# The last two channels of the last down projection in two parts, prompt tokens first

## The chip, the core and the metric

The kernel runs on one NeuronCore of one Trainium2 chip. The metric is the device time of one execution in microseconds (us), first to last instruction and what lies around them. The time before is 2729.76 us, the median of three runs (2729.69 to 2732.67). Lower is better.

## The reference, cut to what matters

One step of a two-layer recurrent decoder with model width 2048. The kernel handles 336 tokens at once: 16 learned meta tokens and 256 prompt tokens (one sequence), and 64 sample tokens (8 sequences of 8). Each layer ends with a gated convolutional feed-forward, and the whole with an RMSNorm over the 2048 channels of a token. The change touches only these last lines:

```python
def conv_ffn(x, buf, g, w_up, w_gate, cw, cb, w_down):
    h = rmsnorm(x, g)
    up = h @ w_up
    upc, new_buf = causal_dwconv(up, buf, cw, cb)
    act = jax.nn.gelu(upc) * (h @ w_gate)
    return x + act @ w_down, new_buf
...
    y = rmsnorm(x, g_final)        # y = x * g / sqrt(mean(x*x) + eps), per token
```

The outputs of concern are `y_prompt` (256 x 2048; meta tokens have no output) and `y_sample` (64 x 2048), float32, 2.1 MB and 0.5 MB.

## The kernel before, in words

Activations lie transposed: `X` has 128 partitions x 16 channel groups ("channels" 0 to 15, each 128 model channels) x 336 tokens. In the token axis columns 0 to 15 are meta (`META` = 16), 16 to 271 prompt (`TP` = 272) and 272 to 335 samples (`T` = 336).

**Matmuls.** Each weight tile is loaded, rounded by ScalarE into `wh` (the high part, fp32r), and VectorE makes the low part `wl`. A product is then three matmuls per 128x128 block: `wh` by high activations, `wh` by low ones, `wl` by high ones (`tile`, L1654 to L1656), each with its own weight load. `RING` = 4 tiles are held at once.

**The last down projection** (`down12`) takes the last 14 blocks of the hidden width, in eight bodies of four tiles; body i makes channels 2i and 2i+1. Tiles j = 0 and 1 are the first seven blocks for the even and the odd channel, j = 2 and 3 the last seven. So a tile has 21 matmuls, and the matmuls of this layer run over columns 16 to 335 (320 tokens). The order on each engine is the order in which the code issues it: no planner, only semaphores between engines.

**Beside it, the output.** When channel c is complete VectorE adds it to `X` (`add_to_x`, L1332). GpSimd squares it and adds the squares to `ssq` (L913, L914; channel 15's squares are made by VectorE in `sql`, L1630). ScalarE multiplies it by the final gain into `yg` (L707), TensorE transposes `yg` in three windows of 128 tokens (`to_tokens`, L1943; windows start at tokens 16, 144 and 208, the last holding the samples in its upper 64 rows), and ScalarE copies the result to `yo` (tokens in partitions, L710).

**The end, in order.** After the last tile TensorE transposes channel 14, sums `ssq` and then `sql` over partitions by matmuls with `ones` (L2101, L2104: per window one column), and transposes channel 15. VectorE makes 1/(mean + eps) (L1632, L1633), ScalarE the root (L896). Then the rows of `yo` are scaled in six pieces, `PIECES` 0 to 5: (window 0, first half of the columns), (0, second half), (1, first), (1, second), (samples, first), (samples, second). VectorE scales pieces 0, 1, 4 (L1638), ScalarE 2, 3, 5 (L901). SyncE issues one store per piece, in the order 0, 2, 1, 3, 4, 5, each after the piece is scaled (L491). The instruction that ends the program waits for all stores.

Of the kernel before, what the change touches and what calls it, by code (L numbers as in the profile page):

```python
# [20 lines left out]
ALU = mybir.AluOpType  # L21
ACT = mybir.ActivationFunctionType
ds = bass.ds

P = 128
# [144 lines left out]
def build(nc, a, o):  # L170
    PH, _ = plan()
    ctx = ExitStack()
    with ctx:
# [3 lines left out]
        def sem(name):  # L177
            return ctx.enter_context(nc.semaphore(name))
# [30 lines left out]
        def union(at, *items):  # L209
# [109 lines left out]
        yg_done, y_t, y_c = sem("yg_done"), sem("y_t"), sem("y_c")  # L319
        sql_made, sums, mean_inv, root, by_dve, by_act = (  # L320
            sem(n) for n in ("sql_made", "sums", "mean_inv", "root", "by_dve", "by_act"))

        block = ctx.enter_context(nc.Block())

# [58 lines left out]
        XAs, CTs = padded(XA, 3 + TP, 3 + LS), padded(CT, 3 + TP, 3 + LS)  # L383
        UPs, CVs = padded(UP, 2 + TP, 2 + LS), padded(CV, 2 + TP, 2 + LS)
        OUT_T = (META, META + P, T - P)
        PIECES = [(t, slice(64 if t == 2 else 0, P), slice(c, c + D // 2)) for t in (0, 1, 2) for c in (0, D // 2)]
        NORMS = {"head": 0, "up00": 1, "win": 2, "up10": 3, "final": 4}

# [47 lines left out]
        @block.sync  # L436
        def _(e):
            e.dma_start(ident[:], a["c_ident"]).then_inc(consts_in, 16)
            for g in (0, 2, 3):
                x_columns(e, g)  # L440

            def load(ph, i, j, w, k0, kn, c):

                e.wait_ge(split, ph.tile(i, j) + 1)
                e.dma_start(raw[:, j % RING, 0:kn * P].rearrange("p (k n) -> p k n", k=kn),
                            w[k0 * P:(k0 + kn) * P, ds(c, P)].rearrange("(k p) n -> p k n", p=P)) \
                    .then_inc(landed[j % RING], 16)

            ph = ph_head = PH["head"]
            columns = [3 * DA, 2 * DA, 4 * DA, 0, 5 * DA, DA]  # L450
            for j in range(12):
                load(ph, 0, j, a["w_in_e"][0], 8 * (j % 2), 8, columns[j // 2])
                if j == RING - 1:
                    e.dma_start(masks[:], a["c_masks"]).then_inc(rows_in, 16)
                    for q, sets in enumerate(rowsets):
                        r = 0
                        for src, n in sets if q else ():
                            e.dma_start(rows[r:r + n, q, :], src).then_inc(rows_in, 16)
                            r += n
            with e.Fori(1, HEADS) as i:  # L460
                for j in range(12):
                    load(ph, i, j, a["w_in_e"][0], 8 * (j % 2), 8, (i + 1) * P + (columns[j // 2] - P))
            for t in range(8):
                load(PH["wout"], t // 4, t % 4, a["w_out_e"][0], 8 * (t // 4), 8, t % 4 * P)
            with e.Fori(2, 8) as i:
                for j in range(4):
                    load(PH["wout"], i, j, a["w_out_e"][0], 8 * (j % 2), 8, i * (2 * P) + (j // 2) * P)

            def ffn(l):
                for p, (f0, n) in enumerate(PARTS):  # L470
                    with e.Fori(0, n) as i:
                        for j in range(4):
                            load(PH[f"up{l}{p}"], i, j, a["w_up" if j < 2 else "w_gate"][l], 8 * (j % 2), 8, i * P + f0 * P)
                    with e.Fori(0, 8) as i:
                        for j in range(4):
                            k0, kn = halves(n)[j // 2]
                            load(PH[f"down{l}{p}"], i, j, a["w_down"][l], f0 + k0, kn, i * (2 * P) + j % 2 * P)

            ffn(0)
            with e.Fori(0, 4) as i:  # L480
                for j in range(4):
                    load(PH["win"], i, j, a["w_in_c"][0], 8 * (j % 2), 8, i * (2 * P) + (j // 2) * P)
            with e.Fori(0, 8) as i:
                for j in range(4):
                    load(PH["glu"], i, j, a["w_glu_v" if j % 2 == 0 else "w_glu_g"][0], 0, 8, i * (2 * P) + (j // 2) * P)
            ffn(1)
            yp, ys = o["y_prompt"][0], o["y_sample"].rearrange("s t d -> (s t) d")
            for n, (done, k) in enumerate(((by_dve, 0), (by_act, 2), (by_dve, 1), (by_act, 3), (by_dve, 4), (by_act, 5))):
                t, rowsl, cols = PIECES[k]
                e.wait_ge(done, n // 2 + 1)  # L490
                e.dma_start(ys[:, cols] if t == 2 else yp[t * P:(t + 1) * P, cols], yo[rowsl, t, cols]).then_inc(out_dma, 16)  # L491


# [1 line left out]
        def _(e):  # L495
# [390 lines left out]
            e.wait_ge(out_dma, 16 * (STORES_A + STORES_F + STORES_C))  # L886
            ffn(1, None)
            ph = PH["down12"]
            for j in range(3):
                to_tokens(ph, 7, j)  # L890
            sc.activation(rs[:, 0:1], ones[:, 0:1], ACT.Sqrt)
            to_tokens(ph, 7, 3)
            for j in range(2):
                to_tokens(ph, 8, j)
            e.wait_ge(mean_inv, 1)
            sc.activation(rs3[:], rs3[:], ACT.Sqrt).then_inc(root, 1)  # L896
            e.wait_ge(root, 1)
            e.wait_ge(y_c, DC + 2)
            for k in (2, 3, 5):
                t, rowsl, cols = PIECES[k]  # L900
                sc.activation(yo[rowsl, t, cols], yo[rowsl, t, cols], ACT.Copy, scale=rs3[rowsl, t:t + 1]).then_inc(by_act, 1)  # L901
            e.wait_ge(out_dma, 16 * (STORES_A + 2 * STORES_F + STORES_C + 6))
            e.wait_ge(s_out, 32 * HEADS + 16)

# [2 lines left out]
        def _(e):  # L907
# [3 lines left out]
            def square(xc):  # L911

                st.then(gp.tensor_tensor(sq[:], xc, xc, ALU.mult))  # L913
                gp.tensor_tensor(ssq[:], ssq[:], sq[:], ALU.add).then_inc(ssq_added, 1)  # L914
# [45 lines left out]
            def squares(ph, groups, norm):  # L960
# [9 lines left out]
                        square(one(X, i * 2 + r))  # L970
                    st.leave(bodies)
                if norm == 4:
                    e.wait_ge(evac, ph.group(bodies, groups[0]) + 1 + BANK_CREDIT)
                    e.wait_ge(ssq_added, norm * DC - 2)
                    square(one(X, DC - 2))

            def load_past(l):
                src = a["state_ffn_conv"][l].rearrange("s r (c p) -> (s r c) p", p=P)
# [93 lines left out]
        def _(e):  # L1072
# [354 lines left out]
            def ffn(l, gnext, norm_next):  # L1427
                for p, (f0, n) in enumerate(PARTS):
# [69 lines left out]
                        down(i)  # L1498
                    if end:
                        for r in range(2):  # L1500
                            add_to_x(ph, ph.bodies - 1, r, 2 + r)

            ffn(0, COL["g_mix"] + DC, 2)
            ph = PH["win"]
# [122 lines left out]
                st.leave(ph.bodies)  # L1627
            ffn(1, None, 4)
            e.wait_ge(evac, PH["down12"].group(7, 1) + 1 + BANK_CREDIT)
            v.tensor_tensor(sql[:], X[:, DC - 1, :], X[:, DC - 1, :], ALU.mult).then_inc(sql_made, 1)  # L1630
            e.wait_ge(sums, 1)
            st.then(v.tensor_scalar(rs3[:], wide[1][:, 0:3, 0:1].rearrange("p t a -> p (t a)"), 1.0 / D, EPS, ALU.mult, ALU.add))  # L1632
            v.reciprocal(rs3[:], rs3[:]).then_inc(mean_inv, 1)  # L1633
            e.wait_ge(root, 1)
            e.wait_ge(y_c, DC + 2)
            for k in (0, 1, 4):
                t, rowsl, cols = PIECES[k]
                v.tensor_scalar(yo[rowsl, t, cols], yo[rowsl, t, cols], rs3[rowsl, t:t + 1], None, ALU.mult).then_inc(by_dve, 1)  # L1638


        @block.tensor
        def _(e):
            pe = nc.tensor

            def tile(ph, i, j, kn, x, b, first, last, halfway=None, t0=0, before_last=None):

                e.wait_ge(split, ph.tile(i, j) + 1 + CREDIT)
                slot, out = j % RING, bank[b][:, t0:T]
                for k in range(kn):
                    if before_last is not None and k == kn - 1:  # L1650
                        before_last()
                    hi, lo = (half[:, t0:T] for half in x(k))
                    whi, wlo = wh[:, slot, k * P:(k + 1) * P], wl[:, slot, k * P:(k + 1) * P]
                    pe.matmul(out, whi, hi, start=first and k == 0, stop=False)  # L1654
                    pe.matmul(out, whi, lo, start=False, stop=False)  # L1655
# [279 lines left out]
                                            BX[:, r, j, 32 * q:32 * q + 32], C0[:, r, 4 * j + q, :], start=r == 0, stop=r == 1)  # L1935
                ins.then_inc(bx_used, 1)

            def to_tokens(i, r):

                e.wait_ge(yg_done, i * 2 + (r - 1))  # L1940
                e.wait_ge(y_c, i * 2 + (r - 1))
                for t, t0 in enumerate(OUT_T):
                    ins = pe.transpose(bank[2 + r][:, t * P:(t + 1) * P], yg[:, r, t0:t0 + P], ident[:])  # L1943
                ins.then_inc(y_t, 1)

            def ffn(l):
                split_h = DC * (2 if l == 0 else 4)
                for p, (f0, n) in enumerate(PARTS):
# [41 lines left out]
                    else:  # L1990
# [5 lines left out]
                        last_turned(l, range(0, 4))  # L1996
                        down(4)
                        last_turned(l, range(4, 7))
                        with e.Fori(5, ph.bodies) as i:
                            down(i)  # L2000

            ffn(0)
            ph = PH["win"]
# [91 lines left out]
            with e.Fori(6, 8) as i:  # L2095
                glu(i)
            ffn(1)
            to_tokens(8, 0)
            e.wait_ge(ssq_added, 4 * DC - 1)
            for t, t0 in enumerate(OUT_T):  # L2100
                pe.matmul(bank[4 + t][:, 0:1], ssq[:, t0:t0 + P], ones[:, 0:1], start=True, stop=False)  # L2101
            e.wait_ge(sql_made, 1)
            for t, t0 in enumerate(OUT_T):
                ins = pe.matmul(bank[4 + t][:, 0:1], sql[:, t0:t0 + P], ones[:, 0:1], start=False, stop=True)  # L2104
            ins.then_inc(sums, 1)
            to_tokens(8, 1)


# [27 lines left out]
```

## Time and profile before

| | |
|---|---|
| median of three runs | 2729.76 us |
| the profiled execution | 2733.15 us |
| its span, first to last instruction | 2731.5 us |
| mean granted TensorE clock | 0.996 of full speed |
| TensorE matmul, weight load (busy share of the span) | 98%, 97% |
| VectorE, ScalarE, GpSimd | 58%, 43%, 16% |
| mean DMA traffic | 140 GB/s |

The profile is of one execution. Busy time of a pipelined TensorE overlaps itself, so 98% says that it is never without work, not that it is at its peak. The pitch (start to start) of two matmuls is what one costs in a dense stretch; the duration shown includes latency that the next one hides.

### The profile page before, as it was taken

The numbers are of one execution on the slowest core, as the hardware profiler recorded it, in microseconds if no ns is written. First come the engines' busy times: TensorE is split into PE (matmuls) and PEld (weight loads), VectorE is DVE, ScalarE is ACT, GpSimd is POOL, SyncE is SP. The second block draws the span as 40 slices with busy tenths as digits, with TensorE's granted clock in tenths as the row PEclk, the third lists the DMA queues.
The fourth block names the chain that finished last, engine by engine and source line by source line (L and its number), as shares of the span: only waits on it lengthen the run. The fifth ranks groups of instructions, "written<-read, shape, count | busy, mean of one in ns | idle before, by whom it ended". The sixth has DMA issues, their size and how long they took to land.

```text
span 2731.5 us, 54085 instructions
## 1 busy us (share of the span) xinstructions
PE 2689.7 (98%) x19939; PEld 2662.5 (97%) x19939; DVE 1588.6 (58%) x2651; ACT 1180.1 (43%) x1534; POOL 442.0 (16%) x533
## 2 busy tenths in 40 slices
PE   7999999999999999999999997999999999999998
PEld 7999999999999999999999996999999999999998
DVE  7666666665554455655556647665554565455554
ACT  5554455434343334435554444543433344334444
POOL 1333333330000000070002571310000000000023
PEclk9999999999999999999999999999999999999999
DMA  6444444555544555445444531555555554555543
GB/s 177 135 135 133 137 142 126 154 147 152 145 138 142 145 144 144 131 141 146 138 140 138 151 102 39 151 146 146 148 146 152 150 150 140 149 157 147 148 139 117
DMA packets 738480, 383.01 MB, mean 140 GB/s; under 512 B 13465, under 2 KB 734661, under 8 KB 738405
## 3 DMA queue, kind: packets, MB, share of 16 engines
q1 hardware_dynamic: 723088, 367.96, 47.2%
q0 software_dynamic: 2560, 7.29, 1.1%
q10 hardware_dynamic: 12756, 6.69, 0.8%
q8 instruction: 55, 0.90, 0.1%
q14 instruction: 21, 0.16, 0.0%
HBM read 373.31 MB, written 8.57 MB: 140 GB/s over the span
## 4 chain that ended last, share of the span: by engine, by line
PE 96%; DVE 3%; issue 0%; ACT 0%; DMA 0%; SPq 0%; DVEq 0%; ACTq 0%
PE banks L1654 31%; PE banks L1655 30%; PE banks L1656 30%; PE banks L1719 1%; PE banks L2045 0%; PE banks L1929 0%; DVE m L1529 0%; DVE m L1531 0%; DVE m L1530 0%; DVE wl L1079 0%; DMA xin<-in_x_sample 0%; DVE h L1135 0%; PE banks L1812 0%; PE banks L1715 0%; PE banks L1810 0%
## 5 line engine op out<-in xcount | busy, mean ns | idle before, releaser
L1079 DVE TENSOR_TENSOR wl<-raw,wh 128x1024 fp32r<-128x1024 f32 x708 | 897.4, 1268 | 793.7 <-ACT wh L502 792.6
L1654 PE MATMUL banks<-h,wh 128*128 128x336 f32 (+2 forms) x3648 | 1156.9, 317 | 2.2 <-DVE wl L1130 2.2
L502 ACT ACTIVATE wh<-raw 128x1024 fp32r<-128x1024 f32 x708 | 749.0, 1058 | 926.8 <-PE banks L1656 908.6
L1655 PE MATMUL banks<-h,wh 128*128 128x336 f32 (+2 forms) x3648 | 1145.8, 314 | 0.0
L1656 PE MATMUL banks<-h,wl 128*128 128x336 f32 (+2 forms) x3648 | 1144.5, 314 | 0.0
L1654 PEld LDWEIGHTS banks<-h,wh 128*128 128x128 f32 x3648 | 685.8, 188 | 9.7 <-issue 7.9
L1655 PEld LDWEIGHTS banks<-h,wh 128*128 128x128 f32 x3648 | 685.8, 188 | 1.7
L1656 PEld LDWEIGHTS banks<-h,wl 128*128 128x128 f32 x3648 | 685.1, 188 | 0.0
L1654 PE MATMUL banks<-act,wh 128*128 128x336 f32 (+2 forms) x1872 | 588.5, 314 | 0.6 <-DVE act L1321 0.6
L1655 PE MATMUL banks<-act,wh 128*128 128x336 f32 (+2 forms) x1872 | 585.3, 313 | 0.0
L1656 PE MATMUL banks<-act,wl 128*128 128x336 f32 (+2 forms) x1872 | 584.8, 312 | 0.0
L1654 PEld LDWEIGHTS banks<-act,wh 128*128 128x128 f32 x1872 | 351.3, 188 | 1.8 <-DVE act L1321 1.2
L1655 PEld LDWEIGHTS banks<-act,wh 128*128 128x128 f32 x1872 | 351.6, 188 | 0.1
L1656 PEld LDWEIGHTS banks<-act,wl 128*128 128x128 f32 x1872 | 351.5, 188 | 0.0
L913 POOL TENSOR_TENSOR sq<-X 128x336 f32 (+1 forms) x63 | 66.7, 1059 | 1284.9 <-DVE X L1332 1209.2
L725 ACT ACTIVATE CV<-UP,prm 128x352 f32<-128x352 f32 x86 | 58.6, 682 | 169.8 <-DVE UP L1449 169.8
L733 ACT ACTIVATE act<-AC 128x336 f32 (+1 forms) x86 | 41.7, 485 | 208.9 <-DVE AC L1465 208.9
L1332 DVE TENSOR_TENSOR X<-X,banks 128x336 f32 (+1 forms) x112 | 56.3, 502 | 101.0 <-PE banks L1656 100.9
L1000 POOL TENSOR_TENSOR tw<-AP 128x32 f32<-128x32 f32 x9 | 3.1, 347 | 565.0 <-DVE AP L1412 564.3
L914 POOL TENSOR_TENSOR ssq<-ssq,sq 128x336 f32<-128x336 f32 x63 | 91.3, 1450 | 4.9
L1468 DVE TENSOR_TENSOR act<-AC,act 128x336 f32 (+1 forms) x86 | 43.7, 508 | 69.5 <-ACT act L733 69.5
L1455 DVE SCALAR_TENSOR_TENSOR CV<-UP,prm,CV 128x352 f32<-128x352 f32 x86 | 50.3, 585 | 48.5 <-ACT CV L725 48.5
(385 smaller groups left out, 1684.3 us busy)
## 6 DMA issues: line engine op xcount, KB each, us to landing
raw<-in_w_up SPq DMA_DIRECT2D x172, 512.0 KB, 3.9
raw<-in_w_gate SPq DMA_DIRECT2D x172, 512.0 KB, 3.9
raw<-in_w_down SPq DMA_DIRECT2D x160, 448.0 KB, 3.7
raw<-in_w_in_e SPq DMA_DIRECT2D x96, 512.0 KB, 3.8
raw<-in_w_out_e SPq DMA_DIRECT2D x32, 512.0 KB, 3.9
raw<-in_w_down SPq DMA_DIRECT2D x32, 512.0 KB, 3.9
raw<-in_w_in_c SPq DMA_DIRECT2D x16, 512.0 KB, 3.7
raw<-in_w_glu_v SPq DMA_DIRECT2D x16, 512.0 KB, 3.9
```

The costliest lines, as they stand in the source:

```text
L502: sc.activation(wh[:, j % RING, :], raw[:, j % RING, :], ACT.Copy).then_inc(rounded, 1)
L725: sc.activation(CV[:, 0:UPW - 2], UP[:, 2:UPW], ACT.Identity, scale=dcol("conv_f_w", i, (l * 3 + 2) * FFC + f0), bias=dcol("conv_f_b", i, ...
L733: sc.activation(part(act, i, 0), AC[:], ACT.Copy).then_inc(act_hi, 1)
L913: st.then(gp.tensor_tensor(sq[:], xc, xc, ALU.mult))
L914: gp.tensor_tensor(ssq[:], ssq[:], sq[:], ALU.add).then_inc(ssq_added, 1)
L1079: v.tensor_tensor(wl[:, j % RING, :], raw[:, j % RING, :], wh[:, j % RING, :].bitcast(F32), ALU.subtract) \
L1332: v.tensor_tensor(one(X, c), one(X, c), bank[ph.bank(r) if b is None else b][:, 0:T], ALU.add).then_inc(evac, 1)
L1455: st.then(v.scalar_tensor_tensor(out=CV[:, 0:UPW - 2], in0=UP[:, 1:UPW - 1], scalar=w(i, 1), in1=CV[:, 0:UPW - 2], op0=ALU.mult, op1=ALU.add))
L1468: v.tensor_tensor(part(act, i, 1), AC[:], part(act, i, 0).bitcast(F32), ALU.subtract).then_inc(act_lo, 1)
L1654: pe.matmul(out, whi, hi, start=first and k == 0, stop=False)
L1655: pe.matmul(out, whi, lo, start=False, stop=False)
L1656: ins = pe.matmul(out, wlo, hi, start=False, stop=last and k == kn - 1)
```

## The change

Body 7 of the last down projection leaves the loop of TensorE and becomes `last_down`. Its four tiles run over the prompt's 256 columns alone (16 to 271). Then the same weights, still in the ring, are run again over the 64 sample columns, into banks 7 and 6 (`late`): `late(0)` and `late(2)` for channel 14, `late(1)` and `late(3)` for channel 15. Between them stand the transposes and the sums of the prompt's two windows; the samples' come after the last of them. Every engine's end is split alike: VectorE adds, squares and inverts the prompt's columns, then the samples'; GpSimd squares channel 14 in two parts; ScalarE makes `yg`, copies and roots in two parts. VectorE now scales pieces 0, 1, 3 and 4, ScalarE 2 and 5, and on VectorE piece 1 stands behind `late(1)` and the samples' squares. The order of the stores is the same.

```diff
+        LATE_BANK = (7, 6)
...
-            for n, (done, k) in enumerate(((by_dve, 0), (by_act, 2), (by_dve, 1), (by_act, 3), (by_dve, 4), (by_act, 5))):
+            for done, n, k in ((by_dve, 1, 0), (by_act, 1, 2), (by_dve, 2, 1), (by_dve, 3, 3), (by_dve, 4, 4), (by_act, 2, 5)):
...
   (ScalarE)
+            scaled(2)
+            for r in range(2):
+                e.wait_ge(late_added, r + 1)
+                sc.activation(yg[:, r, TP:T], X[:, DC - 2 + r, TP:T], ACT.Copy, scale=col("g_final", DC - 2 + r)).then_inc(yg_done, 1)
...
   (VectorE)
+            v.tensor_tensor(sql[:, META:TP], X[:, DC - 1, META:TP], X[:, DC - 1, META:TP], ALU.mult).then_inc(sql_made, 1)
+            late(0)
+            inverse(1, wide[1][:, 0:2, 0:1].rearrange("p t a -> p (t a)"), slice(0, 2))
             e.wait_ge(root, 1)
             e.wait_ge(y_c, DC + 2)
+            scaled(0)
+            late(1)
+            e.wait_ge(late_added, 2)
+            v.tensor_tensor(sql[:, TP:T], X[:, DC - 1, TP:T], X[:, DC - 1, TP:T], ALU.mult).then_inc(sql_made, 1)
+            scaled(1)
+            inverse(2, bank[LATE_BANK[0]][:, 0:1], slice(2, 3))
+            scaled(3)
+            e.wait_ge(root, 2)
+            e.wait_ge(y_c, DC + 4)
+            scaled(4)
...
   (TensorE)
+                for j in range(4):
...
+                    tile(ph, i, j, kn, from_act(k0), ph.bank(j % 2), j < 2, j >= 2, None, META, t1=TP)
...
+                def late(j):
+                    k0, kn = halves(n)[j // 2]
+                    out = bank[LATE_BANK[j % 2]][:, TP:T]
+                    for k in range(kn):
+                        hi, lo = act[:, k0 + k, 0, TP:T], act[:, k0 + k, 1, TP:T]
+                        whi, wlo = wh[:, j, k * P:(k + 1) * P], wl[:, j, k * P:(k + 1) * P]
+                        pe.matmul(out, whi, hi, start=j < 2 and k == 0, stop=False)
+                        pe.matmul(out, whi, lo, start=False, stop=False)
+                        ins = pe.matmul(out, wlo, hi, start=False, stop=j >= 2 and k == kn - 1)
+                    if j >= 2:
+                        ins.then_inc(late_done, 1)
+                late(0)
+                to_tokens(DC // 2, 0, 0, (0, 1))
+                late(2)
+                ...                                  # sums of the prompt's two windows
+                to_tokens(DC // 2, 1, 0, (0, 1))
+                late(1)
+                late(3)
+                to_tokens(DC // 2, 0, 2, (2,))
+                ...                                  # sum of the samples' window
+                to_tokens(DC // 2, 1, 2, (2,))
```

## Rows read from the trace of the kernel before

**Rows 1.** The page, part 1: busy time, share of the span, instructions.

```profile
PE 2689.7 (98%) x19939; PEld 2662.5 (97%) x19939; DVE 1588.6 (58%) x2651; ACT 1180.1 (43%) x1534; POOL 442.0 (16%) x533
```

**Rows 2.** Chain of waits, its last 13 us: start us, us, what.

```profile
2718.08 0.16 PE banks L1656
2718.26 0.51 DVE X L1332
2718.80 0.52 DVE sql L1630
2719.36 0.83 PE banks L2104 x6
2720.19 0.40 PE banks L1943 x3
2720.62 0.49 ACT yo L710
```

**Rows 3.** Timeline, VectorE, ScalarE, GpSimd at the end: start us, us, engine line.

```profile
2721.23 2.20 DVE L1638 TENSOR_SCALAR yo<-yo,rs 128x1024 f32<-128x1024 f32 x3 [0.63 <-ACT rs L896]
...
2716.32 1.28 ACT L891 ACT_TABLE_LOAD   x1
...
2721.23 3.36 ACT L901 ACTIVATE yo<-yo,rs 128x1024 f32<-128x1024 f32 x3
...
2716.59 0.92 POOL L914 TENSOR_TENSOR ssq<-ssq,sq 128x336 f32<-128x336 f32 x1
```

**Rows 4.** Timeline of the store queue (SyncE), first and last of six stores.

```profile
2722.01 0.37 SPq L491 DMA_DIRECT2D out_y_prompt<-yo  x1
...
2726.21 1.30 SPq L491 DMA_DIRECT2D out_y_sample<-yo  x1
```

**Rows 5.** Windows: stretch, its us, each engine's busy us, granted clock, DMA share, GB/s.

```profile
2722.50:2723.00 0.50, 0.00 (x0) 0.00 (x0) 0.47 (x2) 0.50 (x1) 0.00 (x0) 0.53 0.28 115
2723.00:2728.00 5.00, 0.00 (x0) 0.00 (x0) 0.43 (x1) 1.56 (x2) 0.00 (x0) 0.50 1.01 401
2728.50:2730.50 2.00, 0.00 (x0) 0.00 (x0) 0.00 (x0) 0.00 (x0) 0.00 (x0) 0.50 0.96 207
```

**Rows 6.** Timeline of TensorE over the last body (21 matmuls between the first two).

```profile
2705.08 0.31 PE L1654 MATMUL banks<-act,wh 128*128 128x320 f32 x1
...
2708.16 0.49 PE L1943 MATMUL banks<-ident,yg 128*128 128x128 f32 x3
2708.41 0.39 PE L1654 MATMUL banks<-act,wh 128*128 128x320 f32 x1
```

**Rows 7.** Groups by shape, weight loads: xcount, busy us, mean ns, idle before.

```profile
L1655 PEld LDWEIGHTS banks<-act,wh 128*128 128x128 f32 x1872 | 351.6, 188 | 0.1
...
L1934 PEld LDWEIGHTS banks<-C,BX 128*32 128x32 f32 x512 | 4.7, 109 | 0.7 <-issue 0.7
...
L2101 PEld LDWEIGHTS banks<-ones,ssq 128*128 128x128 f32 x6 | 0.7, 192 | 0.0
```

**Rows 8.** Timeline of weight loads: the sums' six, merged.

```profile
2718.28 0.75 PEld L2101 LDWEIGHTS banks<-ones,ssq 128*128 128x128 f32 x6
```

**Rows 9.** Groups by shape, VectorE after 2100 us: a 64-column addition's nearest kin.

```profile
L1465 DVE TENSOR_TENSOR AC<-GT,CV 128x64 f32<-128x64 f32 x28 | 6.1, 219 | 0.0
L1464 DVE TENSOR_TENSOR AC<-GT,CV 128x272 f32<-128x272 f32 x28 | 12.4, 441 | 1.0
```

**Rows 10.** Weight load early in the run, and windows near it.

```profile
25.27 0.33 PEld L1654 LDWEIGHTS banks<-h,wh 128*128 128x128 f32 x1
...
14.00:16.00 2.00, 1.05 (x7) 0.62 (x6) 1.88 (x5) 2.00 (x5) 0.00 (x0) 1.00 1.19 263
18.00:20.00 2.00, 1.32 (x7) 0.81 (x8) 2.00 (x6) 2.00 (x4) 0.00 (x0) 0.79 1.19 290
24.00:26.00 2.00, 2.00 (x9) 2.00 (x8) 2.00 (x5) 2.00 (x6) 0.00 (x0) 0.50 0.18 51
```

**Rows 11.** Chain of waits in a stretch of straight-line narrow matmuls.

```profile
1677.74 1.99 PE banks L2045 x128
1679.73 1.84 issue
```

More of the change, by code:

```diff
@@ L321, in build @@
             sem(n) for n in ("sql_made", "sums", "mean_inv", "root", "by_dve", "by_act"))
+        late_done, late_added = sem("late_done"), sem("late_added")
         block = ctx.enter_context(nc.Block())
@@ L487, in _ @@
             yp, ys = o["y_prompt"][0], o["y_sample"].rearrange("s t d -> (s t) d")
-            for n, (done, k) in enumerate(((by_dve, 0), (by_act, 2), (by_dve, 1), (by_act, 3), (by_dve, 4), (by_act, 5))):
+            for done, n, k in ((by_dve, 1, 0), (by_act, 1, 2), (by_dve, 2, 1), (by_dve, 3, 3), (by_dve, 4, 4), (by_act, 2, 5)):
                 t, rowsl, cols = PIECES[k]
-                e.wait_ge(done, n // 2 + 1)
+                e.wait_ge(done, n)
                 e.dma_start(ys[:, cols] if t == 2 else yp[t * P:(t + 1) * P, cols], yo[rowsl, t, cols]).then_inc(out_dma, 16)
@@ L888, in _, with scaled @@
             ph = PH["down12"]
-            for j in range(3):
+            for j in range(2):
                 to_tokens(ph, 7, j)
[L891 to L894, printed above, removed]
+            for r in range(2):
+                e.wait_ge(evac, ph.group(7, r) + 1 + BANK_CREDIT)
+                e.wait_ge(y_t, DC - 1 + r)
+                sc.activation(yg[:, r, 0:TP], X[:, DC - 2 + r, 0:TP], ACT.Copy, scale=col("g_final", DC - 2 + r)).then_inc(yg_done, 1)
+                if r == 0:
+                    sc.activation(rs[:, 0:1], ones[:, 0:1], ACT.Sqrt)
+            for r in range(2):
+                e.wait_ge(y_t, DC + 1 + r)
+                sc.activation(yo[:, 0:2, (DC - 2 + r) * P:(DC - 1 + r) * P], bank[2 + r][:, 0:2 * P].rearrange("p (t n) -> p t n", t=2), ACT.Copy) \
+                    .then_inc(y_c, 1)
             e.wait_ge(mean_inv, 1)
-            sc.activation(rs3[:], rs3[:], ACT.Sqrt).then_inc(root, 1)
+            sc.activation(rs3[:, 0:2], rs3[:, 0:2], ACT.Sqrt).then_inc(root, 1)
             e.wait_ge(root, 1)
             e.wait_ge(y_c, DC + 2)
-            for k in (2, 3, 5):
+            def scaled(k):
                 t, rowsl, cols = PIECES[k]
                 sc.activation(yo[rowsl, t, cols], yo[rowsl, t, cols], ACT.Copy, scale=rs3[rowsl, t:t + 1]).then_inc(by_act, 1)
+            scaled(2)
+            for r in range(2):
+                e.wait_ge(late_added, r + 1)
+                sc.activation(yg[:, r, TP:T], X[:, DC - 2 + r, TP:T], ACT.Copy, scale=col("g_final", DC - 2 + r)).then_inc(yg_done, 1)
+            for r in range(2):
+                e.wait_ge(y_t, DC + 3 + r)
+                sc.activation(yo[64:P, 2, (DC - 2 + r) * P:(DC - 1 + r) * P], bank[2 + r][64:P, 2 * P:3 * P], ACT.Copy).then_inc(y_c, 1)
+            e.wait_ge(mean_inv, 2)
+            sc.activation(rs3[:, 2:3], rs3[:, 2:3], ACT.Sqrt).then_inc(root, 1)
+            e.wait_ge(root, 2)
+            e.wait_ge(y_c, DC + 4)
+            scaled(5)
             e.wait_ge(out_dma, 16 * (STORES_A + 2 * STORES_F + STORES_C + 6))
@@ L972, in squares @@
                 if norm == 4:
-                    e.wait_ge(evac, ph.group(bodies, groups[0]) + 1 + BANK_CREDIT)
                     e.wait_ge(ssq_added, norm * DC - 2)
-                    square(one(X, DC - 2))
+                    for k, cols in enumerate((slice(0, TP), slice(TP, T))):
+                        if k == 0:
+                            e.wait_ge(evac, ph.group(bodies, groups[0]) + 1 + BANK_CREDIT)
+                        else:
+                            e.wait_ge(late_added, 1)
+                        st.then(gp.tensor_tensor(sq[:, cols], X[:, DC - 2, cols], X[:, DC - 2, cols], ALU.mult))
+                        gp.tensor_tensor(ssq[:, cols], ssq[:, cols], sq[:, cols], ALU.add).then_inc(ssq_added, 1)
             def load_past(l):
@@ L1500, in ffn @@
                         for r in range(2):
-                            add_to_x(ph, ph.bodies - 1, r, 2 + r)
+                            multiplied(ph, ph.bodies - 1, 2 + r)
+                            v.tensor_tensor(X[:, DC - 2 + r, META:TP], X[:, DC - 2 + r, META:TP], bank[ph.bank(r)][:, META:TP], ALU.add) \
+                                .then_inc(evac, 1)
             ffn(0, COL["g_mix"] + DC, 2)
@@ L1629, in _, with late, inverse, scaled @@
             e.wait_ge(evac, PH["down12"].group(7, 1) + 1 + BANK_CREDIT)
[L1630 to L1633, printed above, removed]
+            v.tensor_tensor(sql[:, META:TP], X[:, DC - 1, META:TP], X[:, DC - 1, META:TP], ALU.mult).then_inc(sql_made, 1)
+            def late(r):
+                e.wait_ge(late_done, r + 1)
+                v.tensor_tensor(X[:, DC - 2 + r, TP:T], X[:, DC - 2 + r, TP:T], bank[LATE_BANK[r]][:, TP:T], ALU.add).then_inc(late_added, 1)
+            def inverse(n, sums_of, cols):
+                e.wait_ge(sums, n)
+                st.then(v.tensor_scalar(rs3[:, cols], sums_of, 1.0 / D, EPS, ALU.mult, ALU.add))
+                v.reciprocal(rs3[:, cols], rs3[:, cols]).then_inc(mean_inv, 1)
+            def scaled(k):
+                t, rowsl, cols = PIECES[k]
+                v.tensor_scalar(yo[rowsl, t, cols], yo[rowsl, t, cols], rs3[rowsl, t:t + 1], None, ALU.mult).then_inc(by_dve, 1)
+            late(0)
+            inverse(1, wide[1][:, 0:2, 0:1].rearrange("p t a -> p (t a)"), slice(0, 2))
             e.wait_ge(root, 1)
             e.wait_ge(y_c, DC + 2)
-            for k in (0, 1, 4):
-                t, rowsl, cols = PIECES[k]
-                v.tensor_scalar(yo[rowsl, t, cols], yo[rowsl, t, cols], rs3[rowsl, t:t + 1], None, ALU.mult).then_inc(by_dve, 1)
+            scaled(0)
[5 more added lines that the diff above has]
+            scaled(3)
+            e.wait_ge(root, 2)
+            e.wait_ge(y_c, DC + 4)
+            scaled(4)
         @block.tensor
@@ L1643, in _, with tile @@
             pe = nc.tensor
-            def tile(ph, i, j, kn, x, b, first, last, halfway=None, t0=0, before_last=None):
+            def tile(ph, i, j, kn, x, b, first, last, halfway=None, t0=0, before_last=None, t1=T):
                 e.wait_ge(split, ph.tile(i, j) + 1 + CREDIT)
-                slot, out = j % RING, bank[b][:, t0:T]
+                slot, out = j % RING, bank[b][:, t0:t1]
                 for k in range(kn):
@@ L1651, in tile @@
                         before_last()
-                    hi, lo = (half[:, t0:T] for half in x(k))
+                    hi, lo = (half[:, t0:t1] for half in x(k))
                     whi, wlo = wh[:, slot, k * P:(k + 1) * P], wl[:, slot, k * P:(k + 1) * P]
@@ L1936, in tables, with to_tokens @@
                 ins.then_inc(bx_used, 1)
[L1938 to L1942, printed above, removed]
+            def to_tokens(i, r, later=0, windows=(0, 1, 2)):
+                e.wait_ge(yg_done, i * 2 + (r - 1 + later))
+                e.wait_ge(y_c, i * 2 + (r - 1 + later))
+                for t in windows:
+                    t0 = OUT_T[t]
                     ins = pe.transpose(bank[2 + r][:, t * P:(t + 1) * P], yg[:, r, t0:t0 + P], ident[:])
@@ L1944, in to_tokens, with last_down @@
                 ins.then_inc(y_t, 1)
+            def last_down(ph, n):
+                i = ph.bodies - 1
+                for j in range(4):
+                    k0, kn = halves(n)[j // 2]
+                    if j < 2:
+                        free(ph, i, j)
+                    tile(ph, i, j, kn, from_act(k0), ph.bank(j % 2), j < 2, j >= 2, None, META, t1=TP)
+                    if j < 2:
+                        to_tokens(i, j)
+                def late(j):
+                    k0, kn = halves(n)[j // 2]
+                    out = bank[LATE_BANK[j % 2]][:, TP:T]
[7 more added lines that the diff above has]
+                        ins.then_inc(late_done, 1)
+                e.wait_ge(nc_c, 3 + 2 * 7)
+                late(0)
+                to_tokens(DC // 2, 0, 0, (0, 1))
+                late(2)
+                e.wait_ge(ssq_added, 4 * DC - 1)
+                for t in range(2):
+                    pe.matmul(bank[4 + t][:, 0:1], ssq[:, OUT_T[t]:OUT_T[t] + P], ones[:, 0:1], start=True, stop=False)
+                e.wait_ge(sql_made, 1)
+                for t in range(2):
+                    ins = pe.matmul(bank[4 + t][:, 0:1], sql[:, OUT_T[t]:OUT_T[t] + P], ones[:, 0:1], start=False, stop=True)
+                ins.then_inc(sums, 1)
+                to_tokens(DC // 2, 1, 0, (0, 1))
+                late(1)
+                late(3)
+                to_tokens(DC // 2, 0, 2, (2,))
+                e.wait_ge(ssq_added, 4 * DC)
+                pe.matmul(bank[LATE_BANK[0]][:, 0:1], ssq[:, OUT_T[2]:T], ones[:, 0:1], start=True, stop=False)
+                e.wait_ge(sql_made, 2)
+                pe.matmul(bank[LATE_BANK[0]][:, 0:1], sql[:, OUT_T[2]:T], ones[:, 0:1], start=False, stop=True).then_inc(sums, 1)
+                to_tokens(DC // 2, 1, 2, (2,))
@@ L1998, in ffn @@
                         last_turned(l, range(4, 7))
-                        with e.Fori(5, ph.bodies) as i:
+                        with e.Fori(5, ph.bodies - l) as i:
                             down(i)
+                        if l == 1:
+                            last_down(ph, n)
             ffn(0)
@@ L2097, in _ @@
             ffn(1)
[L2098 to L2106, printed above, removed]
 _INS = ["x_prompt", "x_sample", "state_a_conv", "state_a_h", "state_b_S", "state_c_re", "state_c_im", "state_ffn_conv",
```

## The prediction

> **What bounds the kernel now.** I read the page's busy shares first: TensorE has work for 98% of the span [rows 1], so time is won or lost either in the number and pitch of its matmuls, or at the end, where it has none left. Then the end of the chain of waits [rows 2]: the last matmul of the last tile is done at 2718.24, and from there the chain is all latency: add to X 0.51, squares 0.52, the sums 0.83, transposes 0.40, copy 0.49; scaling begins at 2721.23 [rows 3]. Then the stores [rows 4, 5]: the first is issued at 2722.01. The 0.5 us window at 2722.50 moves 0.28 of a full rate, so data flows from about 2722.86, 0.85 after the issue. It flows at 401 GB/s while the prompt is stored (2.10 MB, 5.24 us) and at 207 GB/s for the samples (0.52 MB, 2.53 us), to about 2730.6. The span ends at 2731.47, 0.87 later. The queue is full from start to finish, although the last store is issued at 2726.21. So behind the last matmul lie 4.6 us until data flows and 7.8 us of data that nothing hides. The change can only gain by letting prompt data flow while TensorE does the samples, and it pays with more matmuls.
>
> **What the change costs on TensorE.** The tiles of the last body: a pitch of 320 columns is (2708.16 - 2705.08)/21 = 0.1467 us [rows 6], at the 2.4 GHz level 0.133 of it columns and 0.013 fixed. With 256 columns that makes 0.107 + 0.013 = 0.120. 84 matmuls save 84 x 0.0267 = 2.24 us, so the prompt's channel 15 is done at 2718.24 - 2.24 = 2716.00.
>
> The late part is 84 matmuls of 64 columns, each with a weight load of its own. No row shows this shape. Ends: columns alone would give 0.027 + 0.013 = 0.040; the wide pitch 0.1467 is the most that a narrower matmul can take at this clock. The nearest rows are those whose weights are the whole 128x128 with almost nothing streamed: the sums of one column, six loads in 0.75 us with 0.19 each, a pitch of (0.75 - 0.19)/5 = 0.112 [rows 8]. Is this one cheaper because its type is fp32r? The load of `wh` takes 188 ns and that of the sums 192, while a load of 32 columns takes 109 [rows 7]: 80 ns for 96 columns more, or 107 for 128. The two kinds agree, so the load itself sets the pitch, and I take 0.112. Late part: 84 x 0.112 = 9.41 us.
>
> The Trainium skill (TensorE: Matmul & The Clock Gate, LDWEIGHTS) gives a load as its columns over 1.2 GHz, which is 107 ns for 128, and so agrees with these rows. Its section on the back-to-back issue gap speaks of about 81 ns for a load and a matmul of 128 columns; by that the late part would be 6.8 us and everything below would end 2.6 us earlier. The rows decide for 0.112.
>
> **The prompt's path.** From 2716.00: `late(0)` 21 x 0.112 = 2.35 to 2718.35. Channel 15's add and squares lie beside it (both wait for nothing else, 0.43 each for 256 columns, nearest row 441 ns for 272 [rows 9]: done at 2716.9). GpSimd's squares of channel 14 also: they ended 2717.51 in the kernel before [rows 3] and now start 1.7 us earlier. ScalarE's root table load, 1.28 us [rows 3], stays hidden in the same place. Two transposes 0.24, `late(2)` 2.35: 2720.94. Sums, now eight loads with the two windows back to back, 8 x 0.112 = 0.90, and the transposes with their latency 0.29 (0.40 less one): 2722.13. The copy of 256 columns 0.40 with its gap, root and gaps 0.15: scaling starts at 2722.68, 1.45 us later than before. So 2.24 was saved and the 1.03 of the add and the squares left the path, while 4.70 of late matmuls came in front.
>
> **The samples' path.** TensorE goes on after the sums and two transposes at 2720.94 + 0.90 + 0.22 = 2722.06 with `late(1)` and `late(3)`, 42 x 0.112 = 4.70, to 2726.76. Now the wait that matters: VectorE's `late(1)` waits for this instant, and behind it in its queue stand pieces 1, 3 and 4, of which 1 and 3 are prompt rows that were ready for scaling at 2723.4. So only pieces 0 (VectorE, 2723.4) and 2 (ScalarE, 1.12 us each [rows 3], 2723.8) are stored beside TensorE's work; the queue then lies idle from about 2726.9. After 2726.76: add 0.22, squares 0.22 [rows 9] and gaps to 2727.26; piece 1 0.75 (three take 2.20 [rows 3]) to 2728.03; the samples' inverse 0.35 (the sum's two loads, its transposes, ScalarE's gain, copies of 64 rows and root fit beside pieces 1 and 3, done by 2728.7); piece 3 to 2729.15; piece 4 to 2729.9; piece 5 on ScalarE by 2729.9 too. Data of piece 1 flows 0.85 after its issue at 2728.05, from 2728.90; each prompt piece is 1.31 us, each sample piece 1.27: 2730.2, 2731.5, 2732.8, 2734.05. With 0.87 to 0.97 behind it the span ends at 2735.0.
>
> **Sum.** 2735.0 against 2731.5: +3.5 us. In terms: data's last stretch is four pieces (5.2 us) from 2728.90 instead of six (7.8) from 2722.86; 6.04 later, 2.6 less. The profiled execution was 2733.15 with 1.65 around its span, 3.4 above the median of the runs; the difference applied to the median gives 2733.3 us.
>
> Waits that cost nothing: SyncE's queue holds only stores, and all four last stores are issued in the order in which they become ready. The added semaphore waits on GpSimd and ScalarE are met long before (`late(0)`'s sum at 2721.2 while the samples' end is at 2726.8). Code that leaves the loop: bounded below by 0 (TensorE ran straight from its loop into the transposes and sums behind it, with loads back to back [rows 8]), above by one fetch pause (below); I take 0.
>
> **Rivals.**
> *The clock falls in the narrow part.* Matmuls of 64 columns stream 27 ns of every 112, a quarter. Early in the run a stretch of seven or so transposes in 2 us kept 1.00 in one window and was granted 0.79 (between 2.4 and 1.2 GHz) four us later; at 0.50 a load's duration is 0.33 [rows 10] instead of 0.19. For it: the late part streams thinly for 10 us. Against: its weight loads are dense, where those stretches had gaps, and the transposes and sums at the end ran with no fall recorded before the engine was idle. Price: if half of the 84 run at twice the pitch, 42 x 0.112 = 4.7 us, all on the samples' path: +8.2 us, 2738. Chance 0.20.
> *Not slower: the narrow matmuls are cheap.* If the load of fp32r weights hides beneath or is shorter than its recorded time, the pitch tends to 0.040: the late part takes 3.4 us, scaling starts at 2719.7, data flows from 2721.25 without a pause and ends at 2729.05, the span at 2730.0: -1.5 us, 2728.3. It decides below a pitch of 0.112 - 3.5/84 = 0.070. For it: pieces 0 and 2 would be hidden as meant. Against: the equal durations of the two kinds of load. Chance 0.13. A rule beside it: the Trainium skill (TensorE: Matmul & The Clock Gate, weight-path perf modes) has a fast weight load for all types but fp32; the 188 ns of this case's fp32r loads show none.
> *A pause for instructions.* In a stretch of straight-line matmuls TensorE ran 128 in 1.99 us and then stood 1.84 with nothing to wait for [rows 11]. `last_down` is straight-line code of some 180. At its pace (128 in 14 us against 128 in 3.83 there) the fetch should keep up; if one pause comes it adds up to 1.8: +5.3 us, 2735.1. Chance 0.08.
> The rest, 0.02, is anything else.
>
> **How the numbers follow.** About 0.2% (5.5 us) is what a measurement of this kernel can tell from no change: 2724.3 to 2735.2. The forecast, +3.5, holds 0.57 and is itself good to about 2 us (pitch 0.107 to 0.12, runs of before differ by 3 us): nearly all of it within 0.2%. So are the cheap matmuls and half of the pause; the clock's case is slower, as is the forecast's upper edge. Faster 0.03, same 0.70, slower 0.27. The range takes in the cheap case below and the clock's above: 2728.0 to 2738.5. The forecast's own is 2731.3 to 2735.3.
>
> **What would show it.** In the changed kernel: pitch of the 256-column matmuls near 0.120 and of the 64-column ones near 0.112; scaling of piece 0 about 6.7 us after the first of the late matmuls; a hole in the store traffic of about 2 us between pieces 2 and 1; VectorE idle about 3.4 us before its late addition, waiting for TensorE; last data about 7.3 us after the last late matmul. Wrong if the 64-column pitch is below 0.07 (then faster), if the granted clock falls before the last late matmul (then slower by more than 0.2%), or if pieces 1 and 3 are stored before `late(3)` ends.

## The result, and the profile after

The changed kernel takes 2742.08 us (median of six runs, 2740.84 to 2743.38) against 2731.38 for the kernel before, measured beside it: 10.7 us slower, a ratio of 1.004 with a 95% interval of 1.003 to 1.0049. The forecast was 2733.3, 3.5 us more than before, range 2728.0 to 2738.5, most likely within 0.2%: wrong in size and in the likeliest case. Slower by more than 0.2% had 0.27.

The place is only the end. The last body of the down projection begins at 2705.08 before [rows 6] and at 2704.50 after (its first matmul of 256 columns, below). From there to the end of the span it is 26.4 us before and 36.1 after: +9.7. This tail, last body to end, is what I compare below: what lies before it differs by up to 2 us from profile to profile, the change edits none of it, and I take that difference for noise. A tail comes from one profile of each kernel. The timed differences are up to 1.7 us away from those of the tails, which is within their intervals (about 2.5 us to each side, or more).

The timeline of TensorE, changed kernel (start us, us, engine line): the first tile of the last body, the first late matmuls, the place where their pitch changes, the last late matmul.

```profile
2704.50 0.28 PE L1707 MATMUL banks<-act,wh 128*128 128x256 f32 x1
2704.62 0.28 PE L1708 MATMUL banks<-act,wh 128*128 128x256 f32 x1
...
2715.09 0.28 PE L2019 MATMUL banks<-act,wh 128*128 128x64 f32 x1
2715.20 0.28 PE L2020 MATMUL banks<-act,wl 128*128 128x64 f32 x1
...
2718.07 0.28 PE L2020 MATMUL banks<-act,wl 128*128 128x64 f32 x1
2718.19 0.34 PE L2018 MATMUL banks<-act,wh 128*128 128x64 f32 x1
2718.34 0.40 PE L2019 MATMUL banks<-act,wh 128*128 128x64 f32 x1
2718.56 0.40 PE L2020 MATMUL banks<-act,wl 128*128 128x64 f32 x1
...
2723.36 0.40 PE L2018 MATMUL banks<-act,wh 128*128 128x64 f32 x1
...
2732.11 0.40 PE L2020 MATMUL banks<-act,wl 128*128 128x64 f32 x1
```

Pitch 0.118 for 256 columns, 0.112 for 64 columns, and from 2718.3 on 0.2133 (the 41 intervals between 2723.36 and 2732.11 give 0.2134). TensorE waits for nothing. The windows of the same kernel show the clock fall at that place (the number behind the busy columns is the granted clock, then DMA share and GB/s):

```profile
2716.00:2718.00 2.00, 2.00 (x21) 2.00 (x20) 0.14 (x1) 0.44 (x2) 0.00 (x0) 1.00 0.00 0
2718.00:2720.00 2.00, 2.00 (x13) 2.00 (x13) 0.00 (x0) 0.18 (x1) 0.00 (x0) 0.57 0.00 0
2720.00:2722.00 2.00, 2.00 (x12) 2.00 (x11) 0.22 (x1) 0.00 (x0) 0.14 (x1) 0.50 0.03 8
...
2726.00:2728.00 2.00, 2.00 (x11) 2.00 (x11) 0.00 (x0) 0.00 (x0) 0.00 (x0) 0.50 1.00 403
2728.00:2730.00 2.00, 2.00 (x12) 2.00 (x11) 0.00 (x0) 0.00 (x0) 0.00 (x0) 0.50 0.25 94
2730.00:2732.00 2.00, 2.00 (x11) 2.00 (x11) 0.00 (x0) 0.00 (x0) 0.00 (x0) 0.50 0.00 0
```

TensorE and its weight loads are 100% busy in every window, and yet the clock goes from 1.00 (2.4 GHz) to 0.50 (1.2 GHz) at about 2718.2, some 3 us after the 64-column matmuls began. The timed runs fit this: their mean granted clock is 0.992 to 0.994 in all six, and 0.994 to 0.997 in the runs of the kernel before. In the kernel before, the clock stayed at 1.00 until TensorE had been out of work for 2 us (0.53 in the window at 2722.50, [rows 5]). The last three windows show the hole in the stores: two prompt pieces are stored by 2728.5, then nothing.

VectorE of the changed kernel, from the scaling of its first piece on:

```profile
2724.25 0.75 DVE L1676 TENSOR_SCALAR yo<-yo,rs 128x1024 f32<-128x1024 f32 x1 [0.68 <-ACT rs L904]
2732.54 0.22 DVE L1665 TENSOR_TENSOR X<-X,banks 128x64 f32<-128x64 f32 x1 [7.54 <-PE banks L2020]
2732.80 0.23 DVE L1685 TENSOR_TENSOR sql<-X 128x64 f32<-128x64 f32 x1
2732.94 0.75 DVE L1676 TENSOR_SCALAR yo<-yo,rs 128x1024 f32<-128x1024 f32 x1
2733.70 0.16 DVE L1670 TENSOR_SCALAR rs<-banks 128x1 f32<-128x1 f32 x1
2733.89 0.16 DVE L1671 RECIPROCAL rs<-rs 128x1 f32<-128x1 f32 x1
2733.97 1.52 DVE L1676 TENSOR_SCALAR yo<-yo,rs 128x1024 f32<-128x1024 f32 x2
```

Its store queue, the second store and the third:

```profile
2725.45 0.42 SPq L493 DMA_DIRECT2D out_y_prompt<-yo  x1
...
2733.72 0.33 SPq L493 DMA_DIRECT2D out_y_prompt<-yo  x1
```

And the end of its chain of waits, which answers to [rows 2]:

```profile
2732.29 0.23 PE banks L2020
2732.54 0.23 DVE X L1665
2732.80 0.24 DVE sql L1685
2733.08 0.58 PE banks L2042 x2
2733.66 0.33 PE banks L1997
2734.01 0.27 ACT yo L919
2734.31 0.21 ACT rs L921
2734.55 1.14 ACT yo L911
```

The same steps as before, on 64 columns, but they start at 2732.54 instead of 2718.26. Scaling begins at 2724.25 instead of 2721.23 [rows 3]; VectorE idles 7.54 us for TensorE (L2020, the last late matmul) with two prompt pieces behind that wait. So the samples' last steps and the storing of four pieces both come after the last late matmul: 8.3 us.

### The profile page after: what moved, and what is told of

Read it like the earlier page. It is cut to its first block, busy times and chain, and to the rows that moved or that the text cites. A ratio compares the mean times of both kernels' runs of the same rounds, so it can differ in the third digit from the quotient of the medians.

```text
span 2740.6 us, 54261 instructions
## 1 busy us (share of the span) xinstructions
PE 2704.7 (99%) x20023; PEld 2676.6 (98%) x20023; DVE 1590.3 (58%) x2657; ACT 1179.3 (43%) x1538; POOL 440.6 (16%) x535
## 4 chain that ended last, share of the span: by engine, by line
PE 89%; issue 5%; DVE 3%; POOL 2%; ACT 1%; DMA 0%; POOLq 0%; SPq 0%; ACTq 0%; DVEq 0%
PE banks L1707 29%; PE banks L1708 28%; PE banks L1709 28%; PE banks L1772 1%; POOL K L961 0%; POOL QF L960 0%; POOL FT L950 0%; PE banks L1982 0%; DMA xin<-in_x_sample 0%; DVE m L1559 0%; DVE m L1561 0%; DVE m L1560 0%; DVE wl L1107 0%; PE banks L1997 0%; DVE h L1163 0%
## 5 line engine op out<-in xcount | busy, mean ns | idle before, releaser
L1707 PE MATMUL banks<-act,wh 128*128 128x336 f32 (+3 forms) x1872 | 588.0, 314 | 0.6 <-DVE act L1349 0.6
L1708 PE MATMUL banks<-act,wh 128*128 128x336 f32 (+3 forms) x1872 | 584.8, 312 | 0.0
L1709 PE MATMUL banks<-act,wl 128*128 128x336 f32 (+3 forms) x1872 | 584.4, 312 | 0.0
L936 POOL TENSOR_TENSOR sq<-X 128x336 f32 x62 | 66.7, 1076 | 1274.7 <-DVE X L1360 1199.0
```

The lines of the kernel that those rows point to most:

```text
L1709: ins = pe.matmul(out, wlo, hi, start=False, stop=last and k == kn - 1)
```

## The experiments

Theory 1: the late part cost its 84 weight loads at a pitch of 0.112, as forecast, and on top of that the clock fell because it streams thinly. Theory 2: the clock falls at this place for another reason. A further rival: the main cost is the order on VectorE, which keeps two prompt pieces behind the late wait. The kernel before was measured anew beside the first four kernels (2731.62 us) and beside the last three (2732.52 us); each ratio is to its own.

**The late part over 256 columns.**

```diff
-                    out = bank[LATE_BANK[j % 2]][:, TP:T]
+                    out = bank[LATE_BANK[j % 2]][:, T - 256:T]
...
-                        hi, lo = act[:, k0 + k, 0, TP:T], act[:, k0 + k, 1, TP:T]
+                        hi, lo = act[:, k0 + k, 0, T - 256:T], act[:, k0 + k, 1, T - 256:T]
```

> The late matmuls run over 256 columns (tokens 80 to 335) instead of 64; the 192 prompt columns more are computed into banks where nobody reads them. Theory 1 (the clock falls because the late part streams thinly, one 64-column matmul per weight load): the granted clock stays 1.00 to the last late matmul, the pitch is 0.118 as in the 256-column tiles, the late part with its sums takes 84 x 0.118 + 1.4 = 11.3 us instead of 17.3, and the kernel is 6 us faster than the changed one, about 2736, still 4 to 5 us slower than before. Theory 2 (the clock falls at this place whatever is streamed, since something else in the tail causes it): the clock falls to 1.2 GHz within about 3 us of the late part, the 256 columns then take 0.21 each or more (0.227 by columns), the late part takes 18 us or more, and the time is 2742 or above.

Measured: 2736.96 us, ratio to before 1.002 (1.0011 to 1.0029); tail 30.0 us. Four times the columns, and 6.1 us less tail. Its windows:

```profile
2718.00:2720.00 2.00, 2.00 (x19) 2.00 (x18) 0.00 (x0) 0.24 (x1) 0.00 (x0) 1.00 0.00 0
2720.00:2722.00 2.00, 2.00 (x20) 2.00 (x19) 0.62 (x4) 0.56 (x3) 0.61 (x2) 1.00 0.04 8
2722.00:2724.00 2.00, 2.00 (x19) 2.00 (x18) 0.68 (x1) 1.31 (x2) 0.00 (x0) 1.00 0.23 94
2724.00:2726.00 2.00, 2.00 (x19) 2.00 (x18) 0.00 (x0) 0.00 (x0) 0.00 (x0) 1.00 0.98 395
```

The clock is 1.00 to the last late matmul. Theory 2 said 2742 or above; it is refuted.

**The late part over 128 columns.** The same edit with 128.

> The late matmuls run over 128 columns, twice the 64; the 64 prompt columns more are not read. At 2.4 GHz this costs nothing, since the weight load sets the pitch (0.112). Theory 1 (thin streaming lowers the clock): if half of the time streaming is enough the clock stays, late part 84 x 0.112 + 1.4 = 10.8 us, 2735.5; if not, the clock falls later than in the changed kernel or at the same place, and the time lies between 2738 and 2742. Theory 2 (the place lowers it): same fall as in the changed kernel, 2742.

Measured: 2736.11 us, ratio 1.0017 (1.0007 to 1.0026); tail 29.35 us.

```profile
2718.00:2720.00 2.00, 2.00 (x20) 2.00 (x19) 0.00 (x0) 0.38 (x1) 0.00 (x0) 1.00 0.00 0
2720.00:2722.00 2.00, 2.00 (x21) 2.00 (x20) 0.55 (x3) 0.35 (x2) 0.61 (x2) 1.00 0.04 8
2722.00:2724.00 2.00, 2.00 (x21) 2.00 (x19) 0.75 (x1) 1.52 (x4) 0.00 (x0) 1.00 0.11 43
2724.00:2726.00 2.00, 2.00 (x21) 2.00 (x19) 0.00 (x0) 0.00 (x0) 0.00 (x0) 1.00 1.00 406
```

The pitch, from two of its late matmuls, ten intervals apart:

```profile
2723.86 0.27 PE L2019 MATMUL banks<-act,wh 128*128 128x128 f32 x1
...
2724.98 0.27 PE L2020 MATMUL banks<-act,wl 128*128 128x128 f32 x1
```

128 columns have the same pitch as 64 (0.112), so the doubled work is free, and the clock stays. This holds beyond the profiles: in all 33 timed runs of the three kernels with 128 or 256 late columns (the third comes below) the mean granted clock is 0.995 to 0.998, in all 11 of the two with 84 late matmuls of 64 columns it is 0.992 to 0.994. This is also the nearest there is to my forecast as it was meant: the changed kernel at full clock. It said a tail of 29.9 us (26.4 + 3.5); 29.35 was measured.

**The prompt's pieces ahead of the late wait**, all else as in the changed kernel, whose clock falls here too.

```diff
             scaled(0)
+            scaled(1)
+            scaled(3)
             late(1)
             e.wait_ge(late_added, 2)
             v.tensor_tensor(sql[:, TP:T], ...).then_inc(sql_made, 1)
-            scaled(1)
             inverse(2, bank[LATE_BANK[0]][:, 0:1], slice(2, 3))
-            scaled(3)
```

> VectorE scales pieces 1 and 3 (prompt) before it waits for the late sum; the rest is the changed kernel, its narrow late matmuls too. Theory 1 (the clock is the main cost, the order on VectorE a small one): the hole in the stores closes, four prompt pieces are stored by about 2731, and the end is set by the samples' chain and two sample pieces: about 1 us less than the changed kernel, 2741. Rival (the prompt pieces behind the late wait are the main cost): the stores no longer queue up behind each other and the end moves by their 2.6 us or more, 2739 or less.

Measured: 2740.76 us, ratio 1.0038 (1.0024 to 1.0051); tail 34.9 us, 1.2 less than the changed kernel's. Of the two costs the order is the small one. The tails say this, here and in the next pair; the timed runs alone can't, since their interval (2738.2 to 2745.6 us) takes in both 2741 and the rival's 2739.

```profile
2716.00:2718.00 2.00, 2.00 (x19) 2.00 (x18) 0.00 (x0) 0.38 (x1) 0.00 (x0) 0.94 0.00 0
2718.00:2720.00 2.00, 2.00 (x12) 2.00 (x11) 0.00 (x0) 0.00 (x0) 0.00 (x0) 0.50 0.00 0
...
2726.00:2728.00 2.00, 2.00 (x12) 2.00 (x11) 0.00 (x0) 0.00 (x0) 0.00 (x0) 0.50 1.01 401
2728.00:2730.00 2.00, 2.00 (x11) 2.00 (x11) 0.00 (x0) 0.00 (x0) 0.00 (x0) 0.50 0.77 305
2730.00:2732.00 2.00, 1.93 (x11) 1.85 (x10) 0.45 (x2) 0.62 (x2) 0.00 (x0) 0.50 0.00 0
```

The hole is closed: the prompt is stored while TensorE works. It gains little, since the samples' chain behind the last late matmul (add 2730.99, scaling 2732.99, store 2733.77) now sets the end by itself.

**Both: 256 columns and the prompt's pieces first.**

> Both: late matmuls over 256 columns and prompt pieces scaled before the late wait. Theory 1: the two add up: 6 us for the clock and 1 to 1.5 for the order, 2734.5 to 2735, so still 3 to 4 us slower than before: the late part costs 84 extra weight loads that hide less than they delay. If it comes out at or below before (2731.4), the split was sound and only the clock and the order spoiled it.

Measured: 2735.94 us, ratio 1.0018 (1.0009 to 1.0027), 1 us above what I expected; tail 29.0 us, 1.0 less than with the columns alone. With the clock kept and the order mended the split still costs 2.6 us of tail.

**The late part left out**, 72 of its 84 matmuls.

```diff
-                    for k in range(kn):
+                    for k in range(1):
...                                              # and the end of the sum with it
```

> The changed kernel with 72 of the 84 late matmuls left out (one block of seven per tile stays), so the samples' part of two channels is not computed in full. All else, the order on VectorE too, stays. It shows what the split would be worth if the samples' part were free. My account: from the first late matmul scaling starts after about 3.3 us (add and squares 0.9, sums 0.9, latency, transposes, copy, root) instead of 9.2, the stores flow without a hole (7.8 us), and the time is 2.5 us below before, 2729. Rival (the hole in the stores or the smaller pieces of work on VectorE and ScalarE cost by themselves): 2731.5 or above.

Measured: 2728.73 us, ratio to before 0.999 (0.9981 to 0.9999); tail 23.4 us, 3.0 less than before. Scaling starts 2.6 us after the first late matmul (3.3 expected). Its first store is issued at 2717.05, 14.0 us after the last body begins (16.9 before). So handling the output in two parts does not by itself make the kernel slower; about 3 us is what the split could win with the samples' part nearly free (twelve of its matmuls still run), and the 72 matmuls cost 8.1 at full clock.

**Only channel 15 in two parts**, channel 14 over 320 columns as before; the late part is then 42 matmuls, six of them in the time in which TensorE waits for the squares, and the prompt's pieces are scaled first. The core of the edit:

```diff
-                    tile(ph, i, j, kn, from_act(k0), ph.bank(j % 2), j < 2, j >= 2, None, META, t1=TP)
+                    tile(ph, i, j, kn, from_act(k0), ph.bank(j % 2), j < 2, j >= 2, None, META, t1=TP if j % 2 else T)
...
-                late(0)
-                to_tokens(DC // 2, 0, 0, (0, 1))
-                late(2)
+                to_tokens(DC // 2, 0)
+                late(1, range(2))
                 ...                                  # sums of the prompt's two windows
                 to_tokens(DC // 2, 1, 0, (0, 1))
-                late(1)
+                late(1, range(2, 7))
                 late(3)
```

With the late part over 128 columns:

> Only channel 15 in two parts: channel 14 runs over 320 columns as before, channel 15 over the prompt first; its late part is 42 matmuls, over 128 columns so that the clock stays, six of them placed where TensorE waits for the squares; VectorE scales the prompt's pieces before it waits for the late sum. My account: the prompt's path gets 1.1 us shorter and pays 0.3 for the sums' extra loads; scaling starts about 0.7 us earlier than before, the samples are ready by 2726 to 2727, when the prompt's data is just stored: 0.5 to 1 us below before, 2730.5 to 2731. Rival (the late part delays the samples' pieces beyond the prompt's data): 2732 to 2733. A clock that falls would show above 2734.

Measured: 2732.49 us, ratio 0.9999 (0.999 to 1.0008); tail 25.1 us, 1.3 less than before. The time is the rival's and not my account's. In its profile scaling starts 14.6 us after the last body begins, 1.6 earlier than before (0.7 expected), and the store queue stands for only 0.2 us between prompt and samples (the window at 2726 below). And over its 64 columns:

> The same with the late part over its 64 columns. If the clock falls some 3 us after the narrow matmuls begin, as in the changed kernel, the last 15 to 20 of 42 run at 0.21 instead of 0.11, 1.5 to 2 us, of which about 1 is hidden behind the prompt's stores: 2731.5 to 2732.5. If it doesn't fall within this shorter part: the same as with 128 columns.

Measured: 2731.71 us, ratio 0.9999 (0.999 to 1.0008); tail 25.6 us. The windows of the 64-column version, then of the one with 128:

```profile
2718.00:2720.00 2.00, 2.00 (x20) 2.00 (x19) 1.58 (x4) 1.60 (x3) 0.00 (x0) 1.00 0.00 0
2720.00:2722.00 2.00, 2.00 (x18) 2.00 (x17) 0.56 (x1) 0.00 (x0) 0.00 (x0) 0.89 0.94 379
...
2725.00:2726.00 1.00, 0.00 (x0) 0.00 (x0) 0.00 (x0) 0.23 (x1) 0.00 (x0) 0.50 0.30 111
```

```profile
2720.00:2722.00 2.00, 2.00 (x20) 2.00 (x20) 1.84 (x3) 0.91 (x1) 0.00 (x0) 1.00 0.31 125
2722.00:2724.00 2.00, 1.59 (x15) 1.51 (x15) 0.45 (x2) 0.35 (x1) 0.00 (x0) 1.00 0.99 397
...
2726.00:2727.00 1.00, 0.00 (x0) 0.00 (x0) 0.00 (x0) 0.02 (x1) 0.00 (x0) 0.50 0.80 274
```

In the narrow one the clock falls with the late part almost done. The steps behind it run slower, the store queue stands for 0.7 us (DMA share 0.30 in the window at 2725) instead of 0.2, and the tail is half a microsecond longer. The profiles' tails are both shorter than before, by 0.8 and 1.3 us; in the timed runs neither kernel differs from before (each interval reaches 0.1% to both sides), nor do they show the half microsecond between the two. So this is a version that loses nothing, not one that is shown to win.

## Why the prediction was wrong

Point by point, by its own steps.

*The tiles of the last body, 84 matmuls saving 2.24 us:* right. The pitch is 0.118 where 0.120 was forecast, and the body takes 10.56 us (2704.50 to 2715.06) where it took 12.99, so 2.43 are saved.

*The late matmuls' pitch of 0.112, set by the weight load:* right as long as the clock was up (2715.09 to 2718.07: 0.112). That 128 columns cost the same as 64, and the sums' single column too [rows 8], shows that it is not the columns that set it; the load is what these three have in common.

*"Late part: 84 x 0.112 = 9.41 us":* this is the step that failed. It took the clock of the tiles before it (1.00) for the whole part. From 2718.3 on, 56 late matmuls and eight loads of the sums ran at 0.2133: 56 x 0.101 + 8 x 0.10 = 6.5 us more. TensorE needed 17.26 us from the first late matmul to the samples' transposes (2715.06 to 2732.32) where the step's terms give 10.8. The two experiments with more columns keep the clock and give back 6.1 us (256) and 6.8 us (128) of tail; with 128 the pitch at full clock is unchanged, so the clock is all that differs there.

*The prompt's path, scaling 1.45 us later than before:* it was 3.0 later, 3.6 counted from the last body; the clock's share again (14 late matmuls and the sums, 2.2 us). With 128 columns it began 17.2 us after the last body against 16.15 before, 1.1 later.

*The samples' path behind `late(3)`:* right. From there to the end 8.24 us were forecast and 8.3 measured (2732.32 to 2740.6). The wait on VectorE, the two pieces behind it and the hole in the stores are where the text had them, but the first and the last are larger, since late matmuls at half the clock lie in them: VectorE idles 7.5 us and not 3.4, and the hole is 6.0 us (2728.5 to 2734.5) and not 2. That the clock might fall before the last late matmul was on the prediction's own list of what would show it wrong. The order's price, which the prediction did not split off, is 1.0 to 1.2 us.

*Rivals.* The falling clock was named as a rival, with its mechanism, at 0.20 and at +8.2 us. It is what happened, and it was mis-sized: I let half of the 84 run slow; it was two thirds, with the sums on top, and on the prompt's path too. The row for it was there: at 0.50 a load takes 0.33 [rows 10]. Both arguments against it were weak. "Its weight loads are dense": in the changed kernel the loads were 100% busy in the window in which the clock fell. And the transposes and sums that kept the clock at the end of the kernel before last 2.3 us (2718.28 to 2720.59), while the narrow stretch had run 3 us when it fell. Cheap matmuls: no, the pitch was 0.112 and not 0.040. A pause for instructions: none seen; the straight-line tail runs without a gap.

*Sum.* With 2.43 saved in the tiles where 2.24 was forecast, and all else as forecast, the change costs +3.3; the clock adds 6.5, together +9.8; the measured tail is +9.7.

## What to carry to other kernels

Splitting a matmul by columns doubles its weight loads, and a narrow one costs its load (0.112 us here, for 1, 64 and 128 columns): price the second part by loads, 84 x 0.112 = 9.4 us here, against what the split can win at best, which was about 3 us. A long stretch of narrow matmuls can cost the clock although the profile shows the engine 100% busy, and then nearly doubles the cost of every matmul behind it (0.2133 for 0.112). If such a stretch is needed, let each matmul stream more columns: here 128 cost no more than 64, 256 cost 0.006 us more, and both kept the clock.

## What the runs showed of the hardware that was not expected

- A busy engine is no guard of its clock: with matmuls of 64 columns back to back, each behind a 128x128 load, it fell from 2.4 to 1.2 GHz; with 128 or 256 columns in the same places it stayed at 2.4. When it falls varies: about 3.2 us after the narrow part began in the changed kernel, 3.8 us in the one with the prompt's pieces first, 5.6 us in the one-channel version with 64 columns (its fall is within the window at 2720).
- The load's cost goes with the granted clock: with 64 columns a pitch of 0.112 us at 1.00 and 0.2133 at 0.50.
- The samples' two stores (64 partitions) move at half the rate of the prompt's (128 partitions): 207 against 401 GB/s in the kernel before [rows 5], 205 in the changed one. The prediction took this from its rows; what causes it was not tried.
